# Two-layer diffusion transformer step: item scores issued two ahead, an earlier router load, and 64-row score halves in two PSUM banks

## What is computed

```python
for l in range(DEPTH):                                   # DEPTH = 2
    sh1, sc1, gt1, sh2, sc2, gt2 = _modulation(silu_lat, w_ada[l], b_ada[l])
    h = _rmsnorm(xs, norm_mix_pre[l]) * (1.0 + sc1) + sh1
    y = _mixer_latent(h, cached, *mix_w, na_rpb[l])      # 4 groups of 4 heads, then w_o
    xs = xs + gt1 * _rmsnorm(y, norm_mix_post[l])
    h = _rmsnorm(xs, norm_ffn_pre[l]) * (1.0 + sc2) + sh2
    xs = xs + gt2 * _rmsnorm(_channel_mixer(h, l, *ffn_w), norm_ffn_post[l])
```

## Time and profile before

| | |
|---|---|
| median of three runs | 1674.35 us |
| the profiled execution: device time | 1674.89 us |
| its span, first to last instruction | 1673.1 us |
| PE busy, share of the span | 94% |
| DVE busy | 71% |
| ACT busy | 58% |
| HBM traffic over the span | 283 GB/s |

### The profile page before, as it was taken

The page is one execution under the profiler, slowest core; times in us unless marked ns, Lnnn a source line. Parts: engine busy times, 40 slices in busy tenths (PEclk is TensorE's granted clock), DMA queues, the critical chain, the costliest instruction groups (busy, mean ns, idle before and its releaser), DMA issues.

```text
span 1673.1 us, 22863 instructions
## 1 busy us (share of the span) xinstructions
PE 1576.5 (94%) x8167; PEld 1295.3 (77%) x8167; DVE 1194.3 (71%) x1014; ACT 976.9 (58%) x958; POOL 89.1 (5%) x142
## 2 busy tenths in 40 slices
PE   5998899999989868999999999999999999999996
PEld 2866789988777747888888888888888888888885
DVE  2556444534556425888888888888888888888885
ACT  4343444434534344776776776776776776776773
POOL 2410040000020010000000000000000000000001
PEclk8999899999989778999999999999999999999998
DMA  9864484577634344998998998998998998998991
GB/s 370 274 195 150 165 257 153 186 240 280 236 117 152 126 152 146 367 368 321 360 371 321 359 369 320 362 365 323 363 363 321 363 365 321 364 365 320 365 366 50
DMA packets 218291, 473.87 MB, mean 283 GB/s; under 512 B 8464, under 2 KB 41536, under 8 KB 218240
## 3 DMA queue, kind: packets, MB, share of 16 engines
q1 hardware_dynamic: 215024, 466.38, 78.3%
q0 software_dynamic: 3216, 6.79, 1.6%
HBM read 470.62 MB, written 2.52 MB: 283 GB/s over the span
## 4 chain that ended last, share of the span: by engine, by line
PE 89%; DVE 4%; ACT 2%; DMA 2%; issue 1%; POOL 1%; POOLq 0%; SPq 0%; DVEq 0%; ACTq 0%
PE ps L1541 22%; PE ps L1546 22%; PE ps L1542 22%; PE ps L1556 3%; PE ps L1557 3%; PE ps L1563 3%; PE ps L1922 2%; PE ps L1751 2%; DMA raw<-in_w_ada 2%; PE ps L1934 1%; PE ps L1715 1%; PE ps L1586 1%; PE ps L1625 1%; DVE w_lo L1060 1%; PE ps L1597 1%
## 5 line engine op out<-in xcount | busy, mean ns | idle before, releaser
L1060 DVE TENSOR_TENSOR w_lo<-raw,w_hi 128x2048 fp32r<-128x2048 f32 (+1 forms) x397 | 903.4, 2284 | 204.7 <-ACT w_hi L712 203.6
L712 ACT ACTIVATE w_hi<-raw 128x2048 fp32r<-128x2048 f32 (+1 forms) x397 | 757.5, 1913 | 254.0 <-PE ps L1542 237.1
L1541 PE MATMUL ps<-w_hi,x_hi 128*128 128x512 f32 (+1 forms) x1216 | 435.2, 370 | 6.5 <-ACT w_hi L712 2.7
L1542 PE MATMUL ps<-w_hi,x_lo 128*128 128x512 f32 (+1 forms) x1216 | 426.7, 363 | 0.0
L1546 PE MATMUL ps<-w_lo,x_hi 128*128 128x512 f32 (+1 forms) x1216 | 284.4, 364 | 0.0
L1541 PEld LDWEIGHTS ps<-w_hi,x_hi 128*128 128x128 f32 x1216 | 228.8, 188 | 47.1 <-issue 7.8
L1542 PEld LDWEIGHTS ps<-w_hi,x_lo 128*128 128x128 f32 x1216 | 228.8, 188 | 36.1
L1546 PEld LDWEIGHTS ps<-w_lo,x_hi 128*128 128x128 f32 x1216 | 206.6, 188 | 39.6
L1541 PE MATMUL ps<-w_hi,h_hi 128*128 128x512 f32 x528 | 207.8, 394 | 0.0
L1542 PE MATMUL ps<-w_hi,h_lo 128*128 128x512 f32 x528 | 207.4, 393 | 0.0
L1546 PE MATMUL ps<-w_lo,h_hi 128*128 128x512 f32 x528 | 141.2, 392 | 0.0
(11 more groups left out here) (242 smaller groups left out, 1213.1 us busy)
## 6 DMA issues: line engine op xcount, KB each, us to landing
raw<-in_moe_w_gate SPq DMA_DIRECT2D x112, 1024.0 KB, 5.2
raw<-in_moe_w_up SPq DMA_DIRECT2D x112, 1024.0 KB, 5.3
raw<-in_moe_w_down SPq DMA_DIRECT2D x112, 1024.0 KB, 5.2
raw<-in_w_ada SPq DMA_DIRECT2D x48, 1024.0 KB, 5.4
raw<-in_w_in SPq DMA_DIRECT2D x20, 960.0 KB, 11.6
raw<-in_ffn_w_gate SPq DMA_DIRECT2D x11, 1024.0 KB, 5.4
raw<-in_ffn_w_up SPq DMA_DIRECT2D x11, 1024.0 KB, 6.4
raw<-in_ffn_w_down SPq DMA_DIRECT2D x11, 1024.0 KB, 5.2
```

The source lines that it names most:

```text
L712: act.activation(split_hi(c, slice(0, width(c))), raw[:, r % NRAW, 0:width(c)], ACT.Copy).then_inc(hi_done, 1)
L1060: dve.tensor_sub(split_lo(c, n), raw[:, raw_of(c) % NRAW, n], split_hi(c, n)).then_inc(lo_done, 1)
L1541: pe.matmul(out, xh, split_hi(c, w), start=start, stop=False, skip_group_check=True)
L1542: last = pe.matmul(out, xl, split_hi(c, w), start=False, stop=False, skip_group_check=True)
```

## The change

It does seven things:

- Scores run two items ahead: items 0 and 1 before the loop, and item i + 2 after the transposes of item i, on PE, DVE and ACT. `probs` gets two buffers per stream (over `x_hi` and `x_lo`).
- The sample stream's score matmuls use 64 rows each instead of 128: two heads with rows 0 to 63 and 64 to 127 stand side by side in banks 4 and 5. For groups C and D the head order changes with that (`head_at`); the bias (D), the rotary part (C2's copy) and the output scaling follow it.
- The order of the late prep steps is C2, C5, C3, C4; the last scores wait for all but C4, and `item_out` of group C waits for C4.
- `ada(l, 20)` and `ada(l, 21)` move from behind the projection into items 8 and 9, and in the weight stream ahead of the third w_o unit.
- The heads of the prompt stream are transposed into banks 0 and 1 instead of 6 and 7, and `out_T` no longer waits for the row of section 4. The third w_o unit is split in item 9, before the split of the transposed heads.
- The router's DMA is issued as soon as attention of layer 1 is over.
- In layer 1 ACT copies the last modulation row and splits the second expert unit before the squares of the sample stream.

```diff
...
 FIRST = [["A", "B0", "B1", "D", "K", "C1"], ["A", "B0", "B1", "D", "Dc", "K", "BM", "C1"]]
-LATER = ["C2", "C3", "C4", "C5"]
+LATER = ["C2", "C5", "C3", "C4"]
 PREP = [FIRST[0] + LATER, FIRST[1] + LATER]
...
             units += win[:2] + ada(1, 8, 9, 10, 11) + win[2:]
-        units += ada(l, 12, 13, 14, 15, 16, 17) + wo[:1] + ada(l, 18) + wo[1:2] + ada(l, 19) + wo[2:]
+        units += ada(l, 12, 13, 14, 15, 16, 17) + wo[:1] + ada(l, 18) + wo[1:2] + ada(l, 19, 20, 21) + wo[2:]
         if l == 0:
-            units += ffn[:2] + ada(0, 20, 21, 22, 23) + ffn[2:23] + ada(1, 4, 5) + ffn[23:26] + ada(1, 6, 7) + ffn[26:29]
+            units += ffn[:2] + ada(0, 22, 23) + ffn[2:23] + ada(1, 4, 5) + ffn[23:26] + ada(1, 6, 7) + ffn[26:29]
             units += ada(1, 0, 1) + ffn[29:31] + ada(1, 2, 3) + ffn[31:]
         else:
-            units += ada(1, 20, 21, 22, 23)
+            units += ada(1, 22, 23)
     return units
...
         x_hi = sb("x_hi", [P, 2, D], F32R)
-        probs = nc.alloc_sbuf_tensor_at("probs", [P, 2, 4, 256], F32, offset=x_hi_at)
+        probs_all = nc.alloc_sbuf_tensor_at("probs", [P, 2, 2, 4, 256], F32, offset=x_hi_at)
         x_lo = sb("x_lo", [P, 2, D], F32R)
...
             if step == "C2":
-                return [(small[:, P * s:P * s + P], ps[:, b, 256:384])] + halves(QZ["C"], 0)
+                return [(small[:, P * s:P * s + P].rearrange("p (a b d) -> p b a d", a=2, b=2),
+                         ps[:, b, 256:384].rearrange("p (b a d) -> p b a d", a=2, b=2))] + halves(QZ["C"], 0)
             if step == "C3":
...

-            return ps[:, 6:8, :] if s == 0 else ps[:, 4:6, :]
+            return ps[:, 4 * s:4 * s + 2, :]

...
             return ps[:, 4:6, :].rearrange("p a (b k) -> p (a b) k", b=2)
+
+        def probs(i):
+
+            return probs_all[:, i // 2 % 2, i % 2, :, :]
+
+        def head_at(it, n):
+
+            return 2 * (n % 2) + n // 2 if it in ("C", "D") else n

...
                     rstd(stat[:, o + 8:o + 12], stat[:, o:o + 4], HD * EPS, drs)
+                if l:
+                    pool.wait_ge(o_evac, 20)
+                    pool.dma_start(rtr, router[0].rearrange("(k p) e -> p k e", p=P)).then_inc(in_rtr, 16)
                 for s in range(2):
...
                         norm_rstd(1, 0, s)
-            pool.wait_ge(x_upd, 6)
-            pool.dma_start(rtr, router[0].rearrange("(k p) e -> p k e", p=P)).then_inc(in_rtr, 16)
             for s in range(2):
...
                 for h in range(4):
-                    src = probs[:, s, h, 0:nk] if biased else score_view(s)[:, h, :]
-                    last = act.activation(probs[:, s, h, 0:nk], src, ACT.Exp, bias=sm[:, s, 4 + h:5 + h],
+                    src = probs(i)[:, h, 0:nk] if biased else score_view(s)[:, h, :]
+                    last = act.activation(probs(i)[:, h, 0:nk], src, ACT.Exp, bias=sm[:, s, 4 + h:5 + h],
                                           scale=1.0 if biased else SCALE[it], accum_out=sm[:, s, 8 + h:9 + h])
...
                     rows(0, 2)
+                for i in range(2):
+                    exps(l, i)
                 for i in range(10):
-                    if i in (4, 8):
-                        rows(l, 2 + i // 4)
-                    exps(l, i)
                     if i in (0, 2, 4, 6):
                         prep(l, len(FIRST[0]) + i // 2)
-                    if i in (6, 8):
-                        split_to(wo_u(l, 0) + i // 2 - 2)
+                    if i + 2 < 10:
+                        exps(l, i + 2)
+                    if i in (3, 7):
+                        rows(l, 3 + i // 4)
+                    if i >= 6:
+                        split_to(wo_u(l, 0) + {6: 1, 7: 1, 8: 2, 9: 3}[i])
                 for s in range(2):
...
                     act.activation(x_hi[:, s, :].rearrange("p (a b) -> p a b", a=2), o_T(s), ACT.Copy).then_inc(o_hi, 1)
-                    if s == 0:
-                        split_to(wo_u(l, 0) + 3)
                 for n in range(2):
...
                     norm_hi(l, 1, 0)
+                else:
+                    rows(l, 5)
+                    split_to(wo_u(l, 2) + 2)
                 norm_sq(l, 1, 1)
-                if l:
-                    rows(l, 5)
                 norm_scale(l, 1, 1)
...
                 if it == "D" and s == 1:
-                    pv = probs[:, 1, :, :]
-                    dve.scalar_tensor_tensor(out=pv[:, :, 0:P], in0=v[:, :, 0:P], scalar=sc,
-                                             in1=bm.rearrange("p (h k) -> p h k", h=4), op0=ALU.mult, op1=ALU.add)
+                    pv = probs(i)
+                    for a in range(2):
+                        dve.scalar_tensor_tensor(out=pv[:, 2 * a:2 * a + 2, 0:P], in0=v[:, 2 * a:2 * a + 2, 0:P], scalar=sc,
+                                                 in1=bm.rearrange("p (b a k) -> p a b k", b=2, a=2)[:, a], op0=ALU.mult, op1=ALU.add)
                     link(dve.tensor_scalar(pv[:, :, P:2 * P], v[:, :, P:2 * P], sc, None, ALU.mult))
...
                 if it not in ("B0", "B1"):
-                    dve.tensor_tensor(xn[:, s, O_COL[it]:O_COL[it] + 256].rearrange("p (h d) -> p h d", h=4), o, r,
-                                      ALU.mult).then_inc(o_evac, 1)
+                    xo = xn[:, s, O_COL[it]:O_COL[it] + 256]
+                    if it == "A":
+                        dve.tensor_tensor(xo.rearrange("p (h d) -> p h d", h=4), o, r, ALU.mult).then_inc(o_evac, 1)
+                    else:
+                        dve.tensor_tensor(xo.rearrange("p (b a d) -> p a b d", b=2, a=2), out_view(s).rearrange("p (a b d) -> p a b d", a=2, b=2),
+                                          sm[:, s, 20:24].rearrange("p (a b) -> p a b", a=2).unsqueeze(3).to_broadcast([P, 2, 2, HD]),
+                                          ALU.mult).then_inc(o_evac, 1)
                     return
...
                 soft_pre(l, 0)
+                soft_pre(l, 1)
                 for i in range(10):
-                    if i + 1 < 10:
-                        soft_pre(l, i + 1)
                     soft_T(l, i)
+                    if i + 2 < 10:
+                        soft_pre(l, i + 2)
                     if i in (1, 3, 5, 7):
...
                                           ALU.mult).then_inc(o_ready, 1)
-                    if i in (6, 8):
-                        split_to(wo_u(l, 0) + i // 2 - 2)
+                    if i >= 6:
+                        split_to(wo_u(l, 0) + {6: 1, 7: 1, 8: 2, 9: 3}[i])
                 for s in range(2):
...
                                    x_hi[:, s, :].rearrange("p (a b) -> p a b", a=2)).then_inc(o_lo, 1)
-                    if s == 0:
-                        split_to(wo_u(l, 0) + 3)
                 gated(l, 0, 0, 0)
...
                 if i >= 8:
-                    pe.wait_ge(prep_evac[s], np_(s) * (l + 1))
-                for h in range(4):
-                    m = 2 * (h % 2) + h // 2 if it == "A" else h
-                    k = nk * (KEYS[it] + (h // 2 if it in ("C", "D") else 0))
-                    last = pe.matmul(v[:, h, :], qz[:, QZ[it], s, m, :], keys[s][:, k:k + nk], start=True, stop=it != "C")
+                    pe.wait_ge(prep_evac[s], np_(s) * (l + 1) - 1)
+
+                def rows(n):
+                    return slice(64 * (n // 2), 64 * (n // 2) + 64) if s else slice(0, P)
+
+                for group in ((0, 2), (1, 3)) if s else ((0,), (1,), (2,), (3,)):
+                    for n in group:
+                        h = head_at(it, n)
+                        m = 2 * (h % 2) + h // 2 if it == "A" else h
+                        k = nk * (KEYS[it] + (h // 2 if it in ("C", "D") else 0))
+                        last = pe.matmul(v[:, n, :], qz[rows(n), QZ[it], s, m, :], keys[s][rows(n), k:k + nk], start=True, stop=it != "C")
                     if it == "C":
                         k = nk * KEYS["rope"]
-                        last = pe.matmul(v[:, h, :], qz[:, QZ["rope"], s, h, :], keys[s][:, k:k + nk], start=False, stop=True)
+                        for n in group:
+                            last = pe.matmul(v[:, n, :], qz[rows(n), QZ["rope"], s, n, :], keys[s][rows(n), k:k + nk], start=False, stop=True)
                 last.then_inc(scores, 1)
...
                     for h in range(4):
-                        last = pe.transpose(ps[:, kb, cols(h, P)], probs[:, i % 2, h, cols(kb, P)], ident())
+                        last = pe.transpose(ps[:, kb, cols(h, P)], probs(i)[:, h, cols(kb, P)], ident())
                 last.then_inc(pT, 1)
...
                 it, s = ITEMS[i // 2], i % 2
-                n = 10 * l + i
-                pe.wait_ge(pt_evac, n + 1)
-                if n:
-                    pe.wait_ge(o_evac, n)
-                for h in range(4):
+                if it == "C":
+                    pe.wait_ge(prep_evac[s], np_(s) * (l + 1))
+                pe.wait_ge(pt_evac, 10 * l + i + 1)
+                if l or i:
```

(19 more changed lines are left out.)

## The result

The changed kernel takes 1652.82 us (median of 4 runs, 1650.81 to 1654.39), the kernel before, run beside it, 1673.94 (4 runs, 1673.44 to 1676.71). The ratio is 0.987, with an interval of [0.9853, 0.9887]: faster by 1.3%. The forecast was 1649.5 in a range of 1641.0 to 1659.5.

The account below looks back on a forecast made before the run. TensorE's own work was taken as the bound (89% of the span), the experts as full. Attention -4.1 and -5.3, routing -17.0 and layer 0 +1.5 gave -24.9 us from 1674.9: 1650.0, less 0.5 for the median, 1649.5; range 1641 to 1659.5.

Parts of the forecast that it names:

- Routing stretch, -17.0: Layer 1, projection to experts: early router DMA and ACT's earlier split bring the logits forward, 17.0 us gained at low clock.
- only the DMA: Rival, routing stretch: earlier splits delay the sample's norm as much as they help, little beyond 7.14 us gained; 1659.5, chance 0.10.
- Attention, -4.1 and -5.3: Attention of layers 0 and 1: busy part (-2.9, -4.1) plus waits (-1.2 each), 4.1 and 5.3 us gained.
- busy time -2.9 and waits -1.2: Attention, layer 0: TensorE's busy part 2.9 us less; waits 8.8 us against 10.05, 1.2 less.
- I take the rows' side, 0.88 us, for five sets: -4.4 us: Attention: two 64-row halves run side by side, each of five sample score sets 0.88 us shorter, 4.4 us gained.
- going in and out: Sample score sets: cost of changing the array's shape, 0.11 us, 1.1 at most over ten sets, kept for the range.
- the turn to the projection: Wait (d), from `out_T` to the projection: stays at 2.4 us; the third w_o split may add 0 to 0.9.
- Layer 0, +1.5: Behind layer 0's projection: idle before the dense part grows from 1.22 to about 3.2 us, clock may fall, 1.5 us lost.
- the middle between two ends: Layer 0's dense part: lower clock costs between 0 and 2.9 us; +1.5 was taken.
- The halves do not overlap: Rival, attention: sample score sets keep 1.78 us, 4.4 us come back per layer less about 1; 1656.5, chance 0.18.
- Nearly gapless: Rival, attention: waits at item 7, `ada(20)` and item 9 better covered, another 3 us a layer; 1643.5, chance 0.17.
- The split rows serialise: Rival, sample scores: halves neither pair nor preload weights, each of 96 records pays; 1683 at 0.35 us each, chance 0.02.

Follow-up runs that it names:

- the tail alone: Kernel before, with only the router's DMA issued early and ACT's last row copy and second expert split ahead of the sample's squares in layer 1: 1661.33 us.
- the version with the clock held: Changed kernel plus unread matmuls in TensorE's waits; sample scores over 128 rows there took 1641.43 us, against 1640.46 with half rows.
- the two with DVE's split last: Extra-matmul kernel, DVE splitting the second expert unit behind its sample norm_h in layer 1: 1638.67 us; also clearing the experts' accumulators before the logits wait: 1642.53.
- the extra matmuls' version: Changed kernel plus 512-column f32 matmuls on constants, result unread, at seven code places in TensorE's waits: 1640.46 us, ratio 0.9799.

## Why the prediction was right, and where it was not

**Routing stretch, -17.0: measured -15.9, right in its mechanism.** On the old time axis (6.47 us later) the sample's squares began at 603.62; the forecast had 603.9. The logits were done at 609.05 + 6.47 = 615.5 (forecast 612.8 at full clock, 616.4 at low), and DVE's split of the third unit at 616.2, which bound (614.7 forecast, and as what binds only at full clock). Against 633.4 of before the choice began 17.3 us earlier, and the gather, at the low clock, took 1.4 of them back: 6.67 us where the kernel before had 5.23 and a wait of 4.42 as well. That term was missing from the sum. So was POOL's step, priced at its usual length: it took 1.0 us more, which the sample's logits, forecast at the low clock and run at the full one, made up for. Five other executions have the same code in this stretch; it took 34.7 to 37.9 us in them, with a gather of 5.35 to 6.72, so the forecast's 35.0 lies within what one execution can give. The rival "only the DMA" is refuted by the tail alone: 13.5 us from the DMA and the order on ACT, and taking either back costs 15 or 4.7.

**Attention, -4.1 and -5.3: measured -4.4 and -5.2, but the terms were not these.** In layer 0 I had busy time -2.9 and waits -1.2; it was -1.3 (55.71 to 54.38) and -3.1 (10.05 to 6.98). In layer 1 I had -4.1 and -1.2; it was -4.9 and -0.3. The step that failed is "**I take the rows' side, 0.88 us, for five sets: -4.4 us**". Its mechanism was wrong: not two heads in two halves but the two records of one head run together. Its size was wrong: 2.7 us, since a set is 0.75 us shorter and not 0.88, and going in and out costs some 0.2 to 0.3 us a set; I had kept 0.11 for that and put it in the range alone. And I let it count fully in the total while I had just written down that DVE's splits are late next: the version with the clock held shows 1.0 us of it. The Trainium skill (TensorEngine Tiling (Array Packing), Key Properties) has the drain at a change of mode; the two timelines agree that something is paid at either edge of a set. The waits were in the right places: item 7 (1.22, forecast 2.5), `ada(20)` (1.56, 1.6), item 9 (1.12 behind products at the low clock in layer 0, 2.16 in layer 1; 2.3), the turn to the projection (3.08, 2.4 to 3.3). Item 7 was mis-sized by my layout. Two errors of opposite sign made a good sum.

**Layer 0, +1.5: measured +1.5 at that place, and 2.1 more elsewhere.** The wait before the dense part is 2.94 us, the first product takes 0.47 at the low clock, and the sample's `norm_T` begins at 212.13:

```profile
207.69 0.47 PE L1573 MATMUL ps<-w_hi,x_hi 128*128 128x256 f32 x1 [2.94 <-DVE x_lo L1136]
...
212.13 1.03 PE L1628 MATMUL ps<-cst,xn 128*128 128x128 f32 x8
```

That is 4.44 us after the first product instead of 2.91. But the middle between two ends was luck: six other executions have the same code and the same wait here, 2.93 or 2.94 us, and the first product took 0.35 or 0.36 us, at full clock, in four of them and 0.55 in two. Not forecast was a second fall later in the dense part (0.91 in the row below, 1.00 in the kernel before), 1.4 us, and one at the first expert product; this is most of what the total missed.

```profile
365.00:385.00 20.00, 17.33 (x132) 15.35 (x131) 7.73 (x6) 7.19 (x7) 0.00 (x0) 0.91 0.68 220
```

But these falls come in some executions and not in others. Between the two attentions the seven executions with this code took 325.1 to 330.9 us, and the one read here is the longest; the median is 328.0, against 327.3 in the kernel before and 327.8 with the tail alone edited. The second fall stands in two of the seven, behind a wait of 2.67 us that all of them have, and the kernel before too. So the 3.6 us are not what the change costs in layer 0; that is too small to tell against this scatter.

**The rivals.** "The halves do not overlap" is refuted in its condition, for the set takes 1.14 us and not 1.78, and in its price: with the sets long again the kernel takes 1651.22 us, not 1656.5. Its doubt was sound all the same, since nothing shows two heads of different halves at once. "Nearly gapless" did not come, the waits stood; with the clock held by extra matmuls the changed kernel reaches 1640.46, below that rival's 1643.5. "The split rows serialise" is refuted by the set of 1.14 us.

**The total.** 1649.5 against 1652.82: 24.9 less 1.1 (routing), 2.1 (layer 0) and 1.6 (first experts), plus 0.55 behind the projection and 0.2 net in attention, less 0.1 at the start, is 20.8. The three that miss are all stretches in which the granted clock was lower than I had taken it, and all three come and go with the execution: from the first expert product to the end, too, the eight executions of the changed kernel and its variants without extra matmuls took 1023.2 to 1025.3 us in the same code. That the total came within 3.3 us is in part luck.

## What to carry to other kernels

Price an edit in the stage where its wait ends last: a DMA of 7 us that was issued late, so that TensorE stood still for 12.8, was worth 15, and 2.7 us of TensorE's work in front of a wait for DVE was worth 1. If a stretch's clock is under 1.00, its idle time can cost twice, once as waiting and again in the products behind it; extra matmuls in the waits gave more here (12.4 us) than all edits to attention (9.6). Place them with a count that ends before the operands come, for at the low clock they take longer and delay the work that they were to help.

## What the runs showed of the hardware that I had not expected

**An fp32 product over 64 rows takes about half the time by itself.** Its two records start together: eight records of 256 columns start within 0.8 us in the half form, in either order of the heads, and within 1.5 us over 128 rows. Two heads in different halves, as the changed kernel has them, gained nothing on top of that.

**A step on POOL waits for DVE's subtraction.** POOL's L603 took 1.28 us beside DVE's L1072, which ran from 597.18 for 2.29 us, to 599.47; POOL's step ended at 599.55. With the subtraction moved it took 0.22, in the run with ACT's split behind the squares and in the two with DVE's split last. The same is in the kernel before, in layer 0 (1.25 us from 200.20, beside L1060 that ended at 201.30). The Trainium skill (SBUF — State Buffer, Who interferes with whom) says that a DVE `tensor_tensor` with both inputs in SBUF contends with GpSimd's reads, and calls the contention on the ports that the two share an exclusive lock. The two ends, 0.08 us apart, agree. In the extra matmuls' version the step took 1.28 us as well, so it comes with the neighbour and not with the execution.

**The same wait doesn't always lower the clock.** Executions of the same instructions differ by up to 2.2 us in one attention: the code of the changed kernel gave 61.36 us at a clock of 0.94 and, with only the tail edited, 63.55 and 63.58 at 0.86 (busy time 54.38, 57.91 and 57.93). Most of the 2 to 7 us between the runs of one kernel here can be this; it also sets what a whole-time comparison can tell. What decides when it falls was not settled.
